# A channel-major SSD scan with paired heads in a two-block sequence model

## The reference

```
xf = x * dt;   cs = cumsum(dt * a) within the chunk, per head
y_diag[l]  = sum over s<=l of (C[l] . B[s]) * exp(cs[l] - cs[s]) * xf[s]
states     = sum over l of B[l] * (xf[l] * exp(cs[last] - cs[l]))
h          = h * exp(cs[last]) + states          (from chunk to chunk)
y_off[l]   = (C[l] . h_previous) * exp(cs[l])
y = (y_diag + y_off + d_skip * x) * silu(z)
y = y * rsqrt(mean of y*y over the group) * norm_w;   out = y @ w_out
```

## Time and profile before

| | us |
|---|---|
| median of 3 runs | 3476.15 |
| lowest and highest | 3470.42, 3476.41 |
| the profiled execution's own time | 3471.82 |
| its span | 3470.2 |
| TensorE busy | 3274.8 |
| VectorE busy | 2051.2 |
| ScalarE busy | 1274.9 |
| GpSimd busy | 401.4 |

### The profile page before, as it was taken

The page is one execution under the profiler, slowest core; times in us unless marked ns, Lnnn a source line. Parts: engine busy times, 40 slices in busy tenths (PEclk is TensorE's granted clock), DMA queues, the critical chain, the costliest instruction groups (busy, mean ns, idle before and its releaser), DMA issues.

```text
span 3470.2 us, 39151 instructions
## 1 busy us (share of the span) xinstructions
PE 3274.8 (94%) x15634; PEld 2582.1 (74%) x15634; DVE 2051.2 (59%) x2723; ACT 1274.9 (37%) x1880; POOL 401.4 (12%) x436
## 2 busy tenths in 40 slices
PE   8998899999899999899999999898879999999998
PEld 7765576778678787677888887685567778888877
DVE  5555546555454545668767665675564677776334
ACT  2554425441433415454223223413423543323123
POOL 1001000120301103010000003240011310000012
PEclk9999999999999999999999999999999999999999
DMA  6210100212402121142222434422064332225232
GB/s 152 48 40 9 50 25 26 63 49 61 67 25 73 43 67 55 37 133 98 73 97 85 138 111 138 130 76 83 1 94 141 110 115 85 85 73 166 89 122 98
DMA packets 344885, 280.36 MB, mean 81 GB/s; under 512 B 52128, under 2 KB 313728, under 8 KB 344416
## 3 DMA queue, kind: packets, MB, share of 16 engines
q1 hardware_dynamic: 322480, 196.30, 19.9%
q0 software_dynamic: 22224, 81.56, 7.3%
HBM read 221.46 MB, written 52.82 MB: 79 GB/s over the span
## 4 chain that ended last, share of the span: by engine, by line
PE 73%; DVE 12%; ACT 7%; issue 5%; DMA 3%; POOL 1%; SPq 1%; ACTq 0%; DVEq 0%; POOLq 0%
PE PS L361 41%; PE PS L2205 12%; PE PA L2205 7%; PE PS L858 2%; PE PA L869 1%; PE PB L1619 1%; DVE WL L325 1%; DMA DEC<-ssd_decay_sums 1%; PE PA L401 1%; PE PB L881 1%; DVE XL L1882 1%; ACT PP L969 1%; DMA WS<-in_ffn_w_out_dram 1%; DVE XST L662 1%; PE PA L1611 1%
## 5 line engine op out<-in xcount | busy, mean ns | idle before, releaser
L361 PE MATMUL PS<-XH,WH 128*128 128x512 f32 x1744 | 608.2, 408 | 37.5 <-DVE XL L1882 19.7
L361 PE MATMUL PS<-XL,WH 128*128 128x512 f32 x1744 | 581.8, 392 | 0.0
L361 PE MATMUL PS<-XH,WL 128*128 128x512 f32 x1744 | 580.9, 392 | 0.0
L318 ACT ACTIVATE WH<-WS 128x1024 fp32r<-128x1024 f32 (+1 forms) x235 | 231.9, 990 | 897.3 <-PE PS L361 851.5
L361 PEld LDWEIGHTS PS<-XH,WH 128*128 128x128 f32 x1744 | 328.7, 190 | 138.8 <-DVE XL L1882 27.5
L361 PEld LDWEIGHTS PS<-XL,WH 128*128 128x128 f32 x1744 | 330.6, 190 | 69.8 <-issue 2.0
L361 PEld LDWEIGHTS PS<-XH,WL 128*128 128x128 f32 x1744 | 330.3, 189 | 70.3
L325 DVE TENSOR_TENSOR WL<-WS,WH 128x1024 fp32r<-128x1024 f32 (+1 forms) x235 | 272.6, 1160 | 184.0 <-ACT WH L318 183.8
L361 PE MATMUL PS<-TQH,WH 128*128 128x512 f32 x448 | 160.9, 394 | 6.2 <-DVE WL L325 6.2
L361 PE MATMUL PS<-TQL,WH 128*128 128x512 f32 x448 | 159.5, 391 | 0.0
L361 PE MATMUL PS<-TQH,WL 128*128 128x512 f32 x448 | 159.4, 391 | 0.0
(11 more groups left out here) (658 smaller groups left out, 6206.5 us busy)
## 6 DMA issues: line engine op xcount, KB each, us to landing
RAW<-in_ffn_w_in_dram SPq DMA_DIRECT2D x36, 1024.0 KB, 6.0
WS<-in_ffn_w_out_dram SPq DMA_DIRECT2D x48, 512.0 KB, 4.1
WS<-in_ssd_w_in_dram SPq DMA_DIRECT2D x40, 512.0 KB, 3.8
DEC<-ssd_decay_sums SPq DMA_DIRECT2D x32, 512.0 KB, 3.7
WS<-in_ffn_w_in_dram SPq DMA_DIRECT2D x32, 512.0 KB, 3.9
TQF<-ffn_hidden POOLq DMA_DIRECT2D x14, 1024.0 KB, 8.0
x_residual<-ACC POOLq DMA_DIRECT2D x6, 2048.0 KB, 7.5
WS<-in_w_mix_in_dram SPq DMA_DIRECT2D x22, 512.0 KB, 3.9
```

What stands on the lines that cost most here:

```text
L318: nc.scalar.activation(WH[:, s, 0:cols], WS[:, s, 0:cols], ACT.Copy).then_inc(W_HI[s], 1)
L361: last = nc.tensor.matmul(PS[s][0:width, c], w[:, s, k * width:(k + 1) * width], x[:, k, c], start=(k == 0 and j == 0), stop=(k == kt - 1 ...
```

## The change

- The y products are turned round. x (64 columns per head) becomes the weights and DEC the moving side with 128 columns, and the output is channel-major. The two heads of a pair write partitions 0 to 63 and 64 to 127 in turn.
- y_off is no product of its own any more. Per chunk a second row set is loaded, exp(cs) per head to all partitions (CDX, two halves of 256 KB, one buffer each), VectorE multiplies it by C (two products of 128x512), and TensorE adds state times this into the same PSUM region, eight more products. The rows are stored once by GpSimd as exponentials of the decay sums (ECROW, `ssd_decays`).
- The load of these rows for chunk c waits for the y products of chunk c - 1; that for chunk 1 of a group is issued with the first two loads of the decay sums.
- skip * x is made by ScalarE, in place in channel-major x (XST), four products of 128x1024 between the exponentials of chunks 0 and 1. VectorE adds PSUM to it (`ssd_add_skip`). The skip vector lies one channel per partition, loaded in two parts.
- There is no turning back. The first half of the next group's first block is worked in chunk 7, ahead of the y products. The gate is multiplied from SBUF by SBUF.
- The new states go to the two halves of PA in turn. GpSimd makes the decayed x of chunk c + 1 behind the mask and ahead of the state's decay, and the state's decay waits for the y products. VectorE adds the state ahead of the chunk before's y.
- The four small loads of group 1 are issued after its last chunk.

```diff
@@ ssd_load_decays (new), called by ssd_sync @@
+    def ssd_load_decays(sp, g, c):
+        if c > 1 or g:
+            sp.wait_ge(SYD, TT * g + (c if c > 1 else 0))
+        if g == 0 and c == 1:
+            sp.wait_ge(EC_OUT, 16)
+        for a in range(2):
+            r = c * SSD_HEADS + g * HPG + a * HPG // 2
+            src = EC_D[r:r + HPG // 2, :].rearrange("h l -> (h l)").unsqueeze(0).broadcast_to([P, HPG // 2 * P])
+            sp.dma_start(CDX[a][:].rearrange("p h l -> p (h l)"), src).then_inc(EC_IN[a], 16)
@@ ssd_sync @@
             for c in range(2):
                 ssd_load_sums(sp, g, c)
+            ssd_load_decays(sp, g, 1)
...
             for c in range(2, TT):
                 ssd_load_sums(sp, g, c)
+                if c > 2:
+                    ssd_load_decays(sp, g, c - 1)
                 if c % 2 == 0:
                     ssd_load(sp, *after[c // 2 - 1])
+            ssd_load_decays(sp, g, TT - 1)
@@ ssd_scan_tensor @@
-            if c:
-                pe.wait_ge(SPREV, 7 * g + c)
-                nc.tensor.matmul(PA[:, 0:GW], CT[:, tok], PREV[:], start=True, stop=True).then_inc(SYO, 1)
             if c < TT - 1:
                 pe.wait_ge(SXDD, 7 * g + c + 1)
-                nc.tensor.matmul(PA[:, HALF:HALF + GW], BTOK[:, c], XDD[c % 2][:], start=True, stop=True).then_inc(SST, 1)
+                if c >= 2:
+                    pe.wait_ge(SPREV, 7 * g + c - 1)
+                nc.tensor.matmul(PA[:, half(c % 2)], BTOK[:, c], XDD[c % 2][:], start=True, stop=True).then_inc(SST, 1)
                 ssd_gate_part(pe, g, c + 1)
+            elif g + 1 < SSD_GROUPS:
+                ssd_in(pe, g + 1, 0, range(0, 4))
             else:
+                pe.wait_ge(SPREV, 7 * g + 6)
                 keep_busy(PA[:, HALF:], 6)
-            pe.wait_ge(SMR, n + 1)
-            if c:
-                pe.wait_ge(SYT_OK, n)
-            for h in range(HPG):
-                last = nc.tensor.matmul(PB[:, HALF + h * SSD_P:HALF + (h + 1) * SSD_P], DEC[n % 2][:, h],
-                                        XTOK[:, c, h * SSD_P:(h + 1) * SSD_P], start=True, stop=True)
-            last.then_inc(SYD, 1)
+            ssd_outputs(pe, g, c)
+
+    def ssd_outputs(pe, g, c):
+        n = TT * g + c
+        pe.wait_ge(SMR, n + 1)
+        if n:
+            pe.wait_ge(SYT_OK, n)
+        if c:
+            pe.wait_ge(SPREV, 7 * g + c)
+            pe.wait_ge(SCTE, 2 * (7 * g + c))
+        for f in range(4):
+            y = [PB[SSD_P * s:SSD_P * s + SSD_P, HALF + f * P:HALF + (f + 1) * P] for s in range(2)]
+            for s in range(2):
+                h = 2 * f + s
+                last = nc.tensor.matmul(y[s], XTOK[:, c, h * SSD_P:(h + 1) * SSD_P], DEC[n % 2][:, h], start=True, stop=(c == 0))
+            for s in range(2 if c else 0):
+                h = 2 * f + s
+                last = nc.tensor.matmul(y[s], PREV[:, h * SSD_P:(h + 1) * SSD_P], CDX[f // 2][:, h % 4], start=False, stop=True)
+        last.then_inc(SYD, 1)
@@ ssd_scalar @@
             ssd_decay(act, g, 0)
+            for f in range(4):
+                nc.scalar.activation(XST[:, f], XST[:, f], ACT.Copy, scale=vec("ssd_d", 4 * g + f)).then_inc(SSKIP, 1)
@@ ssd_vector, behind DEC times the scores @@
                 if c:
-                    (y_diag to SYT, y_off to YOS, new state, YOS to SYT)
+                    ssd_state(dve, g, c)
+                    ssd_add_skip(dve, g, c - 1)
+                    ssd_decayed_c(dve, g, c)
@@ ssd_vector, the gate @@
             for f in range(4):
-                dve.wait_ge(SYTURN, 4 * g + f + 1)
-                v.tensor_tensor(ZT[:, f], ZT[:, f], PAB[f % 2][:], ALU.mult).then_inc(SGATED, 1)
+                v.tensor_tensor(ZT[:, f], ZT[:, f], XST[:, f], ALU.mult).then_inc(SGATED, 1)
@@ new on VectorE @@
+    def ssd_add_skip(dve, g, c):
+        x = XST[:, :, c * P:(c + 1) * P]
+        dve.wait_ge(SYD, TT * g + c + 1)
+        if c == 0:
+            dve.wait_ge(SSKIP, 4 * g + 4)
+        nc.vector.tensor_tensor(x, x, PB[:, HALF:].rearrange("p (f l) -> p f l", f=4), ALU.add).then_inc(SYT_OK, 1)
+
+    def ssd_decayed_c(dve, g, c):
+        b = CT[:, c * P:(c + 1) * P].unsqueeze(1).broadcast_to([P, HPG // 2, P])
+        for a in range(2):
+            dve.wait_ge(EC_IN[a], 16 * (7 * g + c))
+            nc.vector.tensor_tensor(CDX[a][:], CDX[a][:], b, ALU.mult).then_inc(SCTE, 1)
@@ ssd_pool, behind the wait for the turned x @@
-            if g == 1:
-                s5_rate_loads(pool)
+            if g == 0:
+                pool.wait_ge(EC_OUT, 16)
+            ssd_decayed_x(pool, g, 0)
             for c in range(TT):
+                n = TT * g + c
                 if c < TT - 1:
                     ssd_mask(pool, n + 1)
+                if c < TT - 2:
+                    ssd_decayed_x(pool, g, c + 1)
                 if 0 < c < TT - 1:
-                    pool.wait_ge(SYO, 7 * g + c)
+                    pool.wait_ge(SYD, n + 1)
                     tt(heads(PREV[:]), heads(PREV[:]), of_group(CDEC, g, c), ALU.mult).then_inc(SPSC, 1)
-                tt(heads(SYT[:, c]), x, skip, ALU.mult).then_inc(SSK, 1)
+                if g == 1 and c == TT - 1:
+                    s5_rate_loads(pool)
```

More of the change, by code:

```diff
@@ L203, in _build @@
     XST = at("XST", 128, [P, 4, SEQ])
-    SYT = at("SYT", 128, [P, TT, GW])
     BT = at("BT", 144, [P, SEQ])
@@ L208, in _build @@
     PREV = at("PREV", 156, [P, GW])
-    YOS = at("YOS", 158, [P, GW])
+    CDX = [at(f"CDX{a}", 158 if a == 0 else 205, [P, HPG // 2, P]) for a in range(2)]
     ZT = at("ZT", 160, [P, 4, SEQ])
@@ L454, in vec_loads @@
             yield vec("ssd", 34 * g + 30, 4), rows(ins["ssd_norm"][0][g * GW:(g + 1) * GW])
-        for name, src in (("dtb", "ssd_dt_bias"), ("alog", "ssd_a_log"), ("ssd_d", "ssd_d")):
+        for name, src in (("dtb", "ssd_dt_bias"), ("alog", "ssd_a_log")):
             yield vec(name, 0, SSD_HEADS), ins[src].broadcast_to([P, SSD_HEADS])
+        skip = ins["ssd_d"].rearrange("o (q r) -> o r q", r=2)
+        for r in range(2):
+            yield vec("ssd_d", 0, SSD_HEADS // 2)[SSD_P * r:SSD_P * r + SSD_P], skip[:, r].broadcast_to([SSD_P, SSD_HEADS // 2])
     def vecs_sync(eng, n0, n1):
@@ L1433, in dt_vector @@
             dve.wait_ge(SMALL_A, DTD)
-            st(v.tensor_tensor(EDX[:], EDX[:], DTT[:], ALU.mult))
+            st.link(v.tensor_tensor(EDX[:], EDX[:], DTT[:], ALU.mult))
             st.link(v.scalar_tensor_tensor(flat(NCS), PA[:, 0:N_DT], -1.0, s, ALU.mult, ALU.add))
@@ L1456, in dt_pool @@
         pool.dma_start(CS_D.rearrange("(a p) l -> p a l", p=P), CSROW[:]).then_inc(CS_OUT, 16)
+        pool.wait_ge(SMALL_A, DTL + 2)
+        pool.dma_start(EC_D.rearrange("(a p) l -> p a l", p=P), ECROW[:]).then_inc(EC_OUT, 16)
         pool.wait_ge(SMALL_V, DTN)
-    (SSILU, STURN, SCOPY, SCB, SDEC, SMR, SYO, SYD, SST, SXDD, SSK, SPREV, SYT_OK,
-     SYTURN, SGATED, SNS, SYGH, SYGL, CS_OUT) = (sem("ssd_" + n) for n in (
+    (SSILU, STURN, SCOPY, SCB, SDEC, SMR, SYD, SST, SXDD, SPREV, SYT_OK, SSKIP, SCTE,
+     SGATED, SNS, SYGH, SYGL, CS_OUT, EC_OUT) = (sem("ssd_" + n) for n in (
         "silu", "turned", "turned_copied", "cb", "decay",
-        "mixing", "y_off", "y_diag", "states", "x_decayed", "skip", "state_ready", "y_ready",
-        "y_turned", "gated", "normed", "y_hi", "y_lo", "decay_sums_stored"))
+        "mixing", "y_products", "states", "x_decayed", "state_ready", "y_ready", "skip", "c_decayed",
+        "gated", "normed", "y_hi", "y_lo", "decay_sums_stored", "decays_stored"))
     SMASK = sem("ssd_masked")
     CS_IN = [sem(f"ssd_decay_sums_loaded{k}") for k in range(2)]
+    EC_IN = [sem(f"ssd_decays_loaded{a}") for a in range(2)]
     SPSC = sem("ssd_state_decayed")
@@ L1550, in ssd_tensor @@
             ssd_scan_tensor(pe, g)
-            for f in range(4):
-                if f == 2 and ahead:
-                    ssd_in(pe, g + 1, 0, range(0, 4))
-                ssd_turn_back(pe, g, f)
             if ahead:
@@ L1586, in ssd_turn @@
         last.then_inc(STURN, 1)
-    def ssd_turn_back(pe, g, f):
-        if f == 0:
-            pe.wait_ge(SYT_OK, TT * g + TT)
-        if f >= 2:
-            pe.wait_ge(SGATED, 4 * g + f - 1)
-        for t in range(TT):
-            last = nc.tensor.transpose(PAB[f % 2][:, t * P:(t + 1) * P], SYT[:, t, f * P:(f + 1) * P], IDENT[:])
-        last.then_inc(SYTURN, 1)
     def ssd_scan_tensor(pe, g):
@@ L1708, in ssd_vector @@
                 if c:
-                    ssd_add_diagonal(dve, g, c - 1)
-                    dve.wait_ge(SYO, 7 * g + c)
-                    st.link(v.tensor_tensor(heads(YOS[:]), heads(PA[:, 0:GW]), of_group(ECS, g, c), ALU.mult))
-                if c < TT - 1:
-                    dve.wait_ge(SST, 7 * g + c + 1)
-                    if c == 0:
-                        v.tensor_copy(PREV[:], PA[:, HALF:HALF + GW]).then_inc(SPREV, 1)
-                    else:
-                        dve.wait_ge(SPSC, 6 * g + c)
```

(27 more changed lines are left out.)

20 lines of the change are left out of this document (9 added, 11 removed).

## The result

Both kernels were timed in turns. The changed kernel's median is 3448.12 us (4 executions, 3437.83 to 3451.07), that of the kernel before 3476.28 (4 executions, 3470.42 to 3477.8): ratio 0.9915, 95% interval 0.9901 to 0.9929, so 28 us faster. The forecast was 3435, its range 3415 to 3462: right in sign and in the places where it moved time, about 13 us too hopeful. The number measured is that of rival A (3449), and A did come true in part, as the last sections tell.

The account below looks back on a forecast made before the run. TensorE was taken to bound mid-scan, but not the scan's end. Groups 0 to 2 (-28.0), group 3 (+1.0) and rate loads (-14.3) gave -41.3 us: 3430.5 profiled, 3435 as median; range 3415 to 3462.

Parts of the forecast that it names:

- rival A: Scan starts: 2.9 us of idling per group, with waits at the end, brings half clock; 3449 us, chance 0.14.
- Part 2: Middle of a scan, chunks 2 to 5: 0.15 us of waiting, period 8.85 us, -1.3 us a group.
- Part 3: Start of a scan: ScalarE's skip products delay y(1), TensorE idles 2.9 us; +1.8 us a group.
- Part 4: End of a scan: no turning back, half block in the stall; -9.85 us in groups 0 to 2, +0.5 in group 3.
- Part 5: Four slow GpSimd loads moved from the start of group 1's scan to its end: -14.3 us.
- Part 1: The y products: 55 ns a pass instead of 108, 1.75 us with both parts; TensorE's period 8.69 us, 0.49 less.
- Rival C: The y products: pairs don't overlap, 108 ns a pass, +48 us in 28 chunks; 3482 us, chance 0.03.
- Rival E: Group 1: no gain, as the moved loads hit the last chunk's rows or next weights; 3449 us, chance 0.09.
- The edits put at nothing: Small edits such as the early first decay-row load, an exponential, a store and the skip vector's loads: no cost expected.
- Outside the layer: Outside 640 to 1400 us nothing should move; more than 3 us there would make the forecast wrong.

Follow-up runs that it names:

- halves_apart: Changed kernel with all y products of the lower half of the partitions first, then those of the upper; 3479.12 us, ratio 1.0008 to the kernel before.
- x_before_mask: Changed kernel with GpSimd's decayed x of chunk c + 1 ahead of the mask instead of behind it; 3434.42 us, ratio 0.9883 to the kernel before.
- rates_alone: Kernel before with only the four slow loads moved behind the last chunk of group 1's scan; 3460.54 us, ratio 0.9954 to the kernel before.
- rates_back: Changed kernel with the four slow loads back at the start of group 1's scan; 3450.25 us, ratio 0.9921 to the kernel before.
- rows_late: Changed kernel with each group's first decay rows loaded only after y of chunk 0; 3445.6 us, ratio 0.9916 to the kernel before.
- x_behind_decay: Changed kernel with GpSimd's decayed x of chunk c + 1 behind the state's decay instead of ahead; 3495.21 us, ratio 1.006 to the kernel before.

## Why the prediction was right, and where it was short

The pairing, the ends of groups 0 to 2 and the rate loads came at their forecast sizes. What is short of the forecast in the layer is the waiting inside the chunks (Part 2), the scan's start (Part 3) and group 3's end (Part 4), the last two for the most part by half clock, for which the sum had no term. The forecast was -41.3 there and the stretch shows -29.1; by terms, with rounding:

| term | forecast | measured |
|---|---|---|
| Part 3, scan starts, four groups | +7.2 | +12.2 |
| Part 2, chunks 2 to 5, four groups | -5.2 | -0.6 |
| Part 4, ends of groups 0 to 2 | -29.55 | -29.3 |
| Part 4, end of group 3 | +0.5 | +3.0 |
| Part 5, rate loads | -14.3 | -14.3 |

- **Part 1** held: 55 ns a pass, y with both parts 1.75 us, and chunk 6, where nothing waits, takes 8.64 to 8.67 us for a forecast of 8.69. halves_apart shows why: neighbours in the order of issue write different halves. Rival C, 108 ns, is what comes without that: 3482 forecast for it, 3479.12 measured. The Trainium skill's rule that the prediction weighed ("TensorE: Matmul & The Clock Gate", Part 3, overlap only where the row group differs) does not hold here; what the Trainium skill's page "TensorEngine Tiling (Array Packing)", Key Properties, states, that different tiles load weights and multiply in parallel, fits both 55 and 109 ns.
- **Part 2** had the right mechanism and the wrong size. The products with C were ready at t + 7.1 (718.66, y(2) ended at 711.6), forecast t + 7.0. But I took 0.15 us of waiting as a mean over chunks which in fact nearly all lost 0.3 to 0.6 against TensorE's own 8.67: periods of 8.97 to 9.3 and two above (9.43 and 9.51), not 8.85. The sum had TensorE's demand at t + 6.94 and left no room for chance in three sums that all meet within 0.2 us. x_before_mask shows that the collision with GpSimd, put at up to 0.8 us in the prediction, was the larger part of it: without it chunks 2 to 5 gain 5.7 us for the 5.2 forecast. The part's upper bound does not follow from its own terms: 1.2 us late each time is (8.69 + 1.2 - 9.18) x 4 = +2.8 a group, not +4.1.
- **Part 3.** The wait before y(1) was forecast at 2.9 and is 2.9 to 3.6. From the scores of chunk 0 to those of chunk 2 took 18.47 before and takes 21.11, 20.51, 21.76 and 22.70: +2.6, +2.0, +3.3, +4.2, for +1.8 forecast. The rest is for the most part half clock inside and behind y(1) in groups 0, 2 and 3. That is rival A, for which I had argued that 2.9 us is "well short" of 4.86; with a chance of 0.14 it was rated too low. It came true in three groups of four. Against group 1, which had full clock behind the same kind of wait (3.09), they took 0.6, 1.3 and 2.2 us more, 4.1 in all, of which 0.5 is group 3's longer wait; that is less than the 2.6 a group of its price. That the median of 3448 stands next to A's 3449 is in part chance: the chunks' waits and group 3's row sums make up the difference. Why some pauses have half clock behind them and others of the same length do not stays open.
- **Part 4.** From y(5)'s end to the end of the row sums 29.97, 29.9 and 30.05 us: 30.0 was forecast. In groups 1 and 2 the kernel before took a little less than the 39.86 of group 0, so the gain is 29.3 in the three. In group 3 it took 30.5 in place of 28.0, by half clock: 9.82 us of row sums behind a pause of 4.31, where they took 7.13.
- **Part 5.** From group 0 to 1 22.54 us less, of which the group's own terms are +2.04 - 0.52 - 9.79; the rest is -14.3. rates_alone gives 14.2 with nothing else changed. Put back into the changed kernel the loads cost only 10.3, as the wait before y(1) is then hidden by theirs (rates_back). Rival E is excluded.
- **The edits put at nothing.** rows_late confirms the early load. The order of decayed x and decay was put at nothing too, and is right against the order of before, but it is not free to choose (x_behind_decay).
- **Outside the layer** the profiled execution was 5.2 us longer, nearly all of it the scatter ahead of the scan told above. I had said that more than 3 us there would make the forecast wrong; this mark was set too tight for this kernel, as single executions differ by 5 there with the same code. How much of it is in the changed kernel's median is open; no run isolates it. Why attention's clock is lower in some executions is open as well.

## What to carry to other kernels

Where several chains are forecast to meet within a few tenths of a us, as here VectorE's, the load's and TensorE's, count on the worst of them and not on their mean: the changed kernel lost nine tenths of its in-chunk gain that way, and found it again by moving one GpSimd product out of VectorE's window. A term on a slow queue's transfers can be had by itself: half of this change's gain was the place of four small loads. Judge a small edit by the distance between two marks in the trace around the changed code, beside the median.

## What the runs showed of the hardware that was not expected

- fp32 products with 128x64 weights run at 55 ns a pass if neighbours write different halves of the partitions, and at 109 ns if not, though all read the same 128 rows. The difference over this kernel is 31 us.
- The length of a pause alone does not tell whether half clock follows. It stood behind a wait of 2.90 us in one group of x_before_mask and not in two others, not behind 3.09 in the changed kernel's group 1, and behind pauses of 1.11 and 0.64 us close together in seven versions but not in the changed kernel. Only when these, y(1)'s and group 3's last were all filled or shortened was it gone (clock 1.00 over 740 us).
- VectorE products of 128x512 with two inputs, 0.68 us alone, went up to 1.55 us beside one GpSimd product of 1.04.
